# 23 rounded weight slabs written by casting DMAs, and ScalarE's place for what is left, in a hybrid decoder layer

## The chip, the core and the metric

The kernel runs on one core of one Trainium2 chip, as one program without communication. The metric is the device time in microseconds (us); the lower the better. The engines are named as the profile names them: PE is TensorE, DVE is VectorE, ACT is ScalarE, POOL is GpSimd, SP is SyncE.

## What is computed

One decoder layer on 512 tokens of width 1024, all in float32 from outside. The normalised input goes through one wide projection; an HGRN2 recurrence and a sparse attention work on parts of it; their results are lifted, gated, summed and projected out; a squared-ReLU MLP of width 4096 and a last norm follow.

```python
h = rms_norm(x, attn_norm_g[l])
proj = h @ w_in[l]
(hq, hf, hi, hg, cq, ak, av, ik, iw, gate_a, gate_b) = jnp.split(proj, splits, axis=-1)
oa = hgrn2_mixer(hq, hf, hi, lbs[l])
...
cq = rms_norm(cq, q_norm_g[l])
aq = cq @ w_uq[l]
iq = cq @ w_iq[l]
ob = dsa_mixer(aq, iq, iw, ak, av, layer_norm(ik), rel_bias)
mix = jax.nn.sigmoid(gate_a) * (oa @ w_up_hgrn[l]) + jax.nn.sigmoid(gate_b) * (ob @ w_up_attn[l])
x = x + mix @ w_o[l]
```

## The kernel before

**Slabs.** All weights lie in DRAM as one stream of slabs of 128 x 1024 float32 (512 KB). `PLAN` lists the first 55 by kind: hf (slabs 0 to 3), hq (4 to 7), c0 (8 to 11), c1 (12), hi (13 to 16), iq (17), hg (18 to 21), ga (22, 23), uq (24), ga (25 to 30), ua (31 to 34), gb (35 to 42), ub (43 to 46), wo (47 to 54). The MLP's slabs follow in a loop of their own, which the change leaves as it is but for one count of a semaphore.

**Three products per weight.** A matmul in the type float32r sees only a rounded operand. To keep float32's precision each operand is split in a rounded part and a rest, and PE forms hi x hi, hi x lo and lo x hi: 24 matmuls of 512 columns for a slab (of 384 for iq). So each slab n needs, besides the slab itself in `raw`, its rounded form `whi` and the rest `wlo` = raw - whi. There are four buffers of each (`SLOTS`), slab n in number n % 4.

**Who splits.** SP loads `raw` (`load`); for slab n it waits until the split of slab n - 4 is done. ACT copies raw to whi with a cast, in `hi(n)`, once PE is through with slab n - 4 (`used_up`). For most slabs DVE then subtracts (`lo`). For the 23 slabs of `BY_DMA` (18 to 40: hg, ga, uq, ua, and gb 0 to 5) ACT also writes wlo = -whi, in the same `hi(n)`, and POOL issues a DMA that adds raw into wlo (`split_by_dma`). PE waits for that DMA (`split_done`) before its first matmul of the slab.

**Order.** Every engine's program is written out by hand and runs in order; semaphores alone tie the engines together. All walk n over the 55 slabs, and each slab has four parts. In slab n, ACT runs `hi(n + 3)` at part `HI_PART[n]` (0 for n up to 29, 1 from 30), and in each part first empties the banks of that part (`evict`), then does the side work woven into it (`do_side`). POOL begins step n with `split_by_dma(n + 2)` and goes on with its side work of slab n.

```python
HI_PART = [0 if n < n_ua - 1 else 1 for n in range(NPLAN)]
...
for n in range(NPLAN):
    split_by_dma(n - 1 + AHEAD)
    for s in side[n]:
        do_side(s)
```

**Side work that matters here.** In slabs 18 to 21 the indexer: PE writes a bank, ACT turns it to `rel`, DVE adds it into `sc`. In slabs 19 to 23 the recurrence's output: ACT writes `hO` (slabs 20 to 23, one chunk each), and when ACT is through with the slab it squares the chunk (`out_squares`, four squares into `junk`); POOL waits for these squares in its step of that slab to form a reciprocal root (two operations on `small`). Slabs iq and uq fill all four banks of the projections; ACT writes two halves of `iqs` or `aqs` from each bank, DVE the other two, and only then is the bank free for the next slab. In slab 23 ACT starts a DMA of 1 MB (`bt`), ahead of the negation that the change puts there. From slab 30 to 40 attention units are woven in: POOL writes the bias `bm` of a unit, PE forms the unit's logits, DVE adds bm into `tt`, ACT takes the exponential of tt, PE transposes it two units later. bm has two buffers and tt three.

Of the kernel before, what the change touches and what calls it, by code (L numbers as in the profile page):

```python
# [46 lines left out]
SLOTS = 4  # L47
AHEAD = 3


PLAN = ([("hf", j) for j in range(4)] + [("hq", j) for j in range(4)] + [("c0", j) for j in range(4)]
        + [("c1", 0)] + [("hi", j) for j in range(4)] + [("iq", 0)]
        + [("hg", j) for j in range(4)] + [("ga", 0), ("ga", 1), ("uq", 0)] + [("ga", j) for j in range(2, 8)] + [("ua", j) for j in range(4)]
        + [("gb", j) for j in range(8)] + [("ub", j) for j in range(4)] + [("wo", j) for j in range(8)])
NPLAN = len(PLAN)
# [19 lines left out]
def build(nc, x, slabs, vecs, consts, onehot, rel_bias, final_g, out):  # L75
    with ExitStack() as ctx:
# [6 lines left out]
        def sem(name):  # L83
            return ctx.enter_context(nc.semaphore(name))
# [3 lines left out]
        whi = [place(f"whi{s}", 16 + 4 * s, SLAB, F32R) for s in range(SLOTS)]  # L88
# [97 lines left out]
        raw_in = [sem(f"raw_in{s}") for s in range(SLOTS)]  # L186
        br_in = {k: sem(f"br_in{k}") for k in br}
        hi_done, lo_done, lod_done, slab_used = sem("hi_done"), sem("lo_done"), [sem(f"lod_done{q}") for q in range(SLOTS)], sem("slab_used")
        full = [sem(f"full{b}") for b in range(8)]
        free = [sem(f"free{b}") for b in range(8)]  # L190
        const_in, fg_in, y_in, out_done = sem("const_in"), sem("fg_in"), sem("y_in"), sem("out_done")
# [57 lines left out]
        def nextb():  # L249
# [5 lines left out]
        n_hq, n_hi, n_hg, n_ga, n_ua, n_gb, n_ub, n_wo = (  # L255
            AT_SLAB[k, 0] for k in ("hq", "hi", "hg", "ga", "ua", "gb", "ub", "wo"))
# [83 lines left out]

        PARTS = 4
        PART_OF = {"turn": 1, "decay_k": 0, "exp_k": 3, "decay_q": 3, "use_k": 3, "use_q": 2}
        HI_PART = [0 if n < n_ua - 1 else 1 for n in range(NPLAN)]
        LO_PART = [0 if n < n_ua - 1 else 2 for n in range(NPLAN)]
        woven = {}
        for n in range(NPLAN):
# [3 lines left out]
            seen, p, top = 0, 0, 0  # L350
            for s in side[n]:
                if s in BK:
                    p = (2 * seen + 1) * PARTS // (2 * count)
# [25 lines left out]
        BY_DMA = range(n_hg, n_gb + 6)  # L379
        NLO = NPLAN - len(BY_DMA) - 1  # L380

        def split_done(n):

            if n == 1:
                return S["lo1_done"], 1
            if n in BY_DMA:
                return lod_done[n % SLOTS], 16 * len([m for m in BY_DMA if m <= n and m % SLOTS == n % SLOTS])
            return lo_done, n + 1 - sum(m in BY_DMA or m == 1 for m in range(n))

        def used_up(n):  # L390

            if n in by_count:
                return slab_used, by_count[n]
            b, u = c1_bank if tiles[n] == "side" else tiles[n][-1]
            return full[b], u + 1
# [3 lines left out]
        WPB = 4 + len(PRODUCTS)  # L399
# [153 lines left out]
        def _(pool):  # L553
# [29 lines left out]
            for l in range(LEVELS):  # L583
                B, H = 2 << l, 1 << l
                m = mskb[:, 64 * l:64 * l + 64]
# [5 lines left out]
            def do_side(s):  # L591
# [31 lines left out]
                if s[0] == "attn" and s[1] < NU:  # L623
# [13 lines left out]
                    if far:  # L637
# [2 lines left out]
                    pool.tensor_tensor(bm[u % 2][:, far:w], bt3[:, h, WIN - (w - far):WIN], sc_of(i)[:, far:w],  # L640
                                       ALU.add).then_inc(S["bm_done"], 1)

            def split_by_dma(n):

                if n in BY_DMA:
                    s = n % SLOTS
                    pool.wait_ge(S["neg_done"], n - BY_DMA[0] + 1)
                    pool.dma_start(wlo[s][:, :].bitcast(F32), raw[s][:, :], accum_op=ALU.add).then_inc(lod_done[s], 16)

            for n in range(NPLAN):  # L650
                split_by_dma(n - 1 + AHEAD)
                for s in side[n]:
                    do_side(s)
# [21 lines left out]
        def _(act):  # L675
            def hi(n):

                s = n % SLOTS
                act.wait_ge(raw_in[s], 16 * (n // SLOTS + 1))
                if n >= SLOTS:  # L680
                    act.wait_ge(*used_up(n - SLOTS))
                act.copy(whi[s][:, :], raw[s][:, :]).then_inc(hi_done, 1)  # L682
                if n in BY_DMA:
                    act.wait_ge(hi_done, n + 1)
                    act.activation(wlo[s][:, :], whi[s][:, :].bitcast(F32), ACT.Copy, scale=-1.0).then_inc(S["neg_done"], 1)  # L685

            def wait_full(bu):
# [209 lines left out]
            for n in range(NPLAN):  # L897
                for p in range(PARTS):
                    if p == HI_PART[n]:
                        hi(n + AHEAD)  # L900
                    evict(n, p)
                    for s in woven[n][p]:
                        do_side(s)
                for s in side[n]:
                    if s[0] == "out":
                        out_squares(s[1])
# [100 lines left out]
        def _(dve):  # L1007
            def lo(n):

                s = n % SLOTS  # L1010
                dve.wait_ge(hi_done, n + 1)
                dve.tensor_tensor(wlo[s][:, :], raw[s][:, :], whi[s][:, :].bitcast(F32),  # L1012
                                  ALU.subtract).then_inc(lo_done, 1)

# [341 lines left out]
            def lo_op(q, src, it):  # L1356

                s = (NPLAN + q) % SLOTS
                dve.wait_ge(hi_done, it * WPB + (NPLAN + q + 1))
                dve.tensor_tensor(wlo[s][:, :], src[:, :], whi[s][:, :].bitcast(F32), ALU.subtract).then_inc(lo_done, 1)  # L1360

            def lo_in(m, it):
# [565 lines left out]
```

## Time and profile before

| | |
|---|---|
| median of 3 runs | 741.98 us (741.24 to 742.3) |
| the profiled execution, its own time | 742.13 us |
| its span in the profile | 740.4 us |
| PE matmul busy | 720.3 us (97%), 3490 instructions |
| DVE / ACT / POOL busy | 511.4 / 380.3 / 107.5 us |
| granted TensorE clock | 0.998 |
| all 16 DMA engines, bytes | 85.12 MB, 115 GB/s in the mean |

The engines' busy times add up to far more than the span, since they work at once; what counts is which of them the others wait for in a given stretch. The span is 1.7 us shorter than the device time of the same execution. PE's matmuls are pipelined: each is shown as 390 ns long, but one of 512 columns starts every 227 ns, so that 24 take 5.45 us. Starts, not ends, are to be compared.

### The profile page before, as it was taken

Reading aid. Unit: us, or ns where it says so; the run is one execution under the profiler, and the core shown is the slowest. Engines: PE = TensorE matmul, PEld = TensorE weight load, DVE = VectorE, ACT = ScalarE, POOL = GpSimd, SP = SyncE. Lnnn points to the kernel's source line nnn. Section 1 sums busy time; section 2 is a strip of 40 time slices with the busy share of each in tenths; the row PEclk is TensorE's granted clock in tenths of the full one; section 3 lists DMA queues with packets and bytes.
Section 4 is the critical chain, followed back from the end, with each engine's and each line's share of the span. In section 5 each row is a group of like instructions: output and inputs, shape, how many; then the busy total and the mean of one; then the engine's idle time right before and its main releaser. Section 6 shows DMA issues by size and latency. Waiting matters only on the chain.

```text
span 740.4 us, 9813 instructions
## 1 busy us (share of the span) xinstructions
PE 720.3 (97%) x3490; PEld 604.0 (82%) x3490; DVE 511.4 (69%) x791; ACT 380.3 (51%) x595; POOL 107.5 (15%) x145
## 2 busy tenths in 40 slices
PE   5999999999999999999999999999999999999996
PEld 4788878788788888888888888888888888888885
DVE  4676996658798852336635696868768595968964
ACT  6463645877755666443313654545363544545442
POOL 3421241012213356200200100000000000000002
PEclk9999999999999999999999999999999999999999
DMA  8456124524977544112722333241505052332102
GB/s 296 145 100 154 58 91 102 133 74 100 257 184 171 143 114 114 58 58 85 256 86 81 147 114 113 86 142 57 170 11 198 17 156 70 113 114 85 30 1 113
DMA packets 25051, 85.12 MB, mean 115 GB/s; under 512 B 2712, under 2 KB 4920, under 8 KB 25016
## 3 DMA queue, kind: packets, MB, share of 16 engines
q1 hardware_dynamic: 19104, 67.87, 27.1%
q0 software_dynamic: 3312, 12.06, 8.7%
q10 hardware_dynamic: 2600, 4.72, 2.9%
q8 instruction: 22, 0.36, 0.2%
q14 instruction: 13, 0.11, 0.0%
HBM read 68.91 MB, written 3.67 MB: 98 GB/s over the span
## 4 chain that ended last, share of the span: by engine, by line
PE 93%; ACT 4%; DVE 1%; issue 1%; DMA 0%; POOL 0%; POOLq 0%; SPq 0%; ACTq 0%; DVEq 0%
PE bank L1513 19%; PE bank L1514 19%; PE bank L1515 19%; PE bank L1559 8%; PE bank L1563 8%; PE bank L1560 8%; PE bank L1744 2%; PE bank L1521 2%; PE bank L1652 2%; PE bank L1530 1%; PE bank L1726 1%; ACT whi L682 1%; PE bank L1725 1%; ACT wlo L685 1%; ACT iqs L744 0%
## 5 line engine op out<-in xcount | busy, mean ns | idle before, releaser
L1513 PE MATMUL bank<-hTh,whi 128*128 128x512 f32 (+1 forms) x264 | 102.9, 390 | 0.5 <-DVE hTl L1038 0.5
L1515 PE MATMUL bank<-hTh,wlo 128*128 128x512 f32 (+1 forms) x264 | 102.8, 389 | 0.0
L1514 PE MATMUL bank<-hTl,whi 128*128 128x512 f32 (+1 forms) x264 | 102.8, 389 | 0.0
L682 ACT CAST whi<-raw 128x1024 fp32r<-128x1024 f32 x58 | 60.4, 1042 | 41.2 <-PE bank L1515 40.6
L1559 PE MATMUL bank<-hTh,whi 128*128 128x512 f32 x192 | 77.8, 405 | 2.2 <-DVE aqs L1068 1.5
L1515 PE MATMUL bank<-whi,al 128*128 128x512 f32 x196 | 76.3, 389 | 0.0
L1514 PE MATMUL bank<-wlo,ah 128*128 128x512 f32 x196 | 76.3, 389 | 0.0
L1513 PE MATMUL bank<-whi,ah 128*128 128x512 f32 x196 | 76.3, 389 | 0.0
L1563 PE MATMUL bank<-hTl,whi 128*128 128x512 f32 x192 | 75.1, 391 | 0.0
L1560 PE MATMUL bank<-hTh,wlo 128*128 128x512 f32 x192 | 74.9, 390 | 0.0
L1012 DVE TENSOR_TENSOR wlo<-raw,whi 128x1024 fp32r<-128x1024 f32 x34 | 45.3, 1335 | 26.1 <-ACT whi L682 26.1
L927 ACT ACTIVATE rt<-bank 128x512 f32<-128x512 f32 x32 | 19.2, 599 | 85.8 <-PE bank L1515 85.8
L1513 PEld LDWEIGHTS bank<-hTh,whi 128*128 128x128 f32 (+1 forms) x264 | 49.2, 186 | 11.4 <-issue 0.7
L1515 PEld LDWEIGHTS bank<-hTh,wlo 128*128 128x128 f32 (+1 forms) x264 | 49.2, 186 | 10.7
L1514 PEld LDWEIGHTS bank<-hTl,whi 128*128 128x128 f32 (+1 forms) x264 | 49.2, 186 | 10.6
L918 ACT CAST whi<-raw 128x1024 fp32r<-128x1024 f32 x29 | 29.8, 1049 | 50.3 <-PE bank L1515 50.3
L1360 DVE TENSOR_TENSOR wlo<-br,whi 128x1024 fp32r<-128x1024 f32 x32 | 39.1, 1222 | 18.8 <-ACT whi L923 18.6
L665 POOL TENSOR_SCALAR small<-small 128x1 f32<-128x1 f32 x4 | 0.8, 191 | 310.0 <-ACT junk L697 310.0
L1393 DVE TENSOR_TENSOR acc<-bank,acc 128x512 f32<-128x512 f32 x70 | 45.1, 688 | 0.0
L1559 PEld LDWEIGHTS bank<-hTh,whi 128*128 128x128 f32 x192 | 36.2, 189 | 9.7 <-issue 3.4
L1513 PEld LDWEIGHTS bank<-whi,ah 128*128 128x128 f32 x196 | 36.8, 188 | 7.7
L1515 PEld LDWEIGHTS bank<-whi,al 128*128 128x128 f32 x196 | 36.8, 188 | 7.6
(245 smaller groups left out, 1623.6 us busy)
## 6 DMA issues: line engine op xcount, KB each, us to landing
raw<-slabs SPq DMA_DIRECT2D x87, 512.0 KB, 3.4
br<-slabs SPq DMA_DIRECT2D x32, 512.0 KB, 3.4
wlo<-raw POOLq DMA_DIRECT2D x23, 512.0 KB, 4.6
xs<-x SPq DMA_DIRECT2D x4, 512.0 KB, 5.3
y<-x ACTq DMA_DIRECT2D x1, 2048.0 KB, 8.9
bias_rows<-rbias ACTq DMA_DIRECT2D x1, 1536.0 KB
out<-ys SPq DMA_DIRECT2D x3, 512.0 KB, 2.6
bt<-bias_rows ACTq DMA_DIRECT2D x1, 1024.0 KB, 6.0
```

The source lines that it names most:

```text
L682: act.copy(whi[s][:, :], raw[s][:, :]).then_inc(hi_done, 1)
L918: act.copy(whi[s][:, :], raw[s][:, :]).then_inc(hi_done, 1)
L927: act.activation(rt[m % 2][:, :], bank[m][:, :], ACT.Relu).then_inc(free[m], 1)
L1012: dve.tensor_tensor(wlo[s][:, :], raw[s][:, :], whi[s][:, :].bitcast(F32), ALU.subtract).then_inc(lo_done, 1)
L1360: dve.tensor_tensor(wlo[s][:, :], src[:, :], whi[s][:, :].bitcast(F32), ALU.subtract).then_inc(lo_done, 1)
L1393: dve.tensor_tensor(a_, bank[b][:, :], a_, ALU.add).then_inc(free[b], 1)
L1513: pe.matmul(dst, lh, rh, start=start, stop=False)
L1514: pe.matmul(dst, lh, rl, start=False, stop=False)
L1515: return pe.matmul(dst, ll, rh, start=False, stop=stop)
L1559: pe.matmul(dst, wh[:, k, c0:c0 + P], hi_[:, k, t0:T], start=k == 0, stop=False)
L1560: pe.matmul(dst, wl[:, k, c0:c0 + P], hi_[:, k, t0:T], start=False, stop=False)
L1563: ins = pe.matmul(dst, wh[:, k, c0:c0 + P], lo_[:, k, t0:T], start=False, stop=k == kt - 1)
```

## The change

For the 23 slabs of `BY_DMA` ACT no longer casts. POOL issues a DMA that reads the slab a second time from DRAM and writes it to whi, with a cast from float32 to float32r (`round_by_dma`), at the start of its step n for slab n + 3, before `split_by_dma(n + 2)`. It may start once PE is through with slab n - 1. ACT's negation is a step of its own (`neg`), now at the end of the last part of slab n, and waits for the casting DMA (`cast_done`). The accumulating DMA also waits for `raw_in`. `HI_PART` is 3 for iq and uq. The slabs 20 and 27, which it would place there, are among the 23, so that this part of the diff moves nothing by itself: what takes the cast and the negation from ahead of these banks is the new `neg`. The counts of `hi_done` go down by the 23 casts.

```diff
--- before.py
+++ after.py
@@ -186,6 +186,7 @@
         raw_in = [sem(f"raw_in{s}") for s in range(SLOTS)]
         br_in = {k: sem(f"br_in{k}") for k in br}
         hi_done, lo_done, lod_done, slab_used = sem("hi_done"), sem("lo_done"), [sem(f"lod_done{q}") for q in range(SLOTS)], sem("slab_used")
+        cast_done = [sem(f"cast_done{q}") for q in range(SLOTS)]
         full = [sem(f"full{b}") for b in range(8)]
         free = [sem(f"free{b}") for b in range(8)]
         const_in, fg_in, y_in, out_done = sem("const_in"), sem("fg_in"), sem("y_in"), sem("out_done")
@@ -340,7 +341,8 @@
 
         PARTS = 4
         PART_OF = {"turn": 1, "decay_k": 0, "exp_k": 3, "decay_q": 3, "use_k": 3, "use_q": 2}
-        HI_PART = [0 if n < n_ua - 1 else 1 for n in range(NPLAN)]
+        HI_PART = [3 if PLAN[n][0] in ("iq", "uq") else 0 if n < n_ua - 1 else 1 for n in range(NPLAN)]
+        NEG_PART = [3] * NPLAN
         LO_PART = [0 if n < n_ua - 1 else 2 for n in range(NPLAN)]
         woven = {}
         for n in range(NPLAN):
@@ -384,8 +386,15 @@
             if n == 1:
                 return S["lo1_done"], 1
             if n in BY_DMA:
-                return lod_done[n % SLOTS], 16 * len([m for m in BY_DMA if m <= n and m % SLOTS == n % SLOTS])
+                return lod_done[n % SLOTS], of_dma(n)
             return lo_done, n + 1 - sum(m in BY_DMA or m == 1 for m in range(n))
+
+        def of_dma(n):
+            return 16 * len([m for m in BY_DMA if m <= n and m % SLOTS == n % SLOTS])
+
+        def rounded(n):
+
+            return hi_done, n + 1 - sum(m in BY_DMA for m in range(n))
 
         def used_up(n):
 
@@ -640,14 +649,23 @@
                     pool.tensor_tensor(bm[u % 2][:, far:w], bt3[:, h, WIN - (w - far):WIN], sc_of(i)[:, far:w],
                                        ALU.add).then_inc(S["bm_done"], 1)
 
+            def round_by_dma(n):
+
+                if n in BY_DMA:
+                    s = n % SLOTS
+                    pool.wait_ge(*used_up(n - SLOTS))
+                    pool.dma_start(whi[s][:, :], slabs[n]).then_inc(cast_done[s], 16)
+
             def split_by_dma(n):
 
                 if n in BY_DMA:
                     s = n % SLOTS
                     pool.wait_ge(S["neg_done"], n - BY_DMA[0] + 1)
+                    pool.wait_ge(raw_in[s], 16 * (n // SLOTS + 1))
                     pool.dma_start(wlo[s][:, :].bitcast(F32), raw[s][:, :], accum_op=ALU.add).then_inc(lod_done[s], 16)
 
             for n in range(NPLAN):
+                round_by_dma(n + AHEAD)
                 split_by_dma(n - 1 + AHEAD)
                 for s in side[n]:
                     do_side(s)
@@ -675,13 +693,19 @@
         def _(act):
             def hi(n):
 
+                if n in BY_DMA:
+                    return
                 s = n % SLOTS
                 act.wait_ge(raw_in[s], 16 * (n // SLOTS + 1))
                 if n >= SLOTS:
                     act.wait_ge(*used_up(n - SLOTS))
                 act.copy(whi[s][:, :], raw[s][:, :]).then_inc(hi_done, 1)
+
+            def neg(n):
+
+                s = n % SLOTS
                 if n in BY_DMA:
-                    act.wait_ge(hi_done, n + 1)
+                    act.wait_ge(cast_done[s], of_dma(n))
                     act.activation(wlo[s][:, :], whi[s][:, :].bitcast(F32), ACT.Copy, scale=-1.0).then_inc(S["neg_done"], 1)
 
             def wait_full(bu):
@@ -901,6 +925,8 @@
                     evict(n, p)
                     for s in woven[n][p]:
                         do_side(s)
+                    if p == NEG_PART[n]:
+                        neg(n + AHEAD)
                 for s in side[n]:
                     if s[0] == "out":
                         out_squares(s[1])
@@ -1008,7 +1034,7 @@
             def lo(n):
 
                 s = n % SLOTS
-                dve.wait_ge(hi_done, n + 1)
+                dve.wait_ge(*rounded(n))
                 dve.tensor_tensor(wlo[s][:, :], raw[s][:, :], whi[s][:, :].bitcast(F32),
                                   ALU.subtract).then_inc(lo_done, 1)
 
@@ -1356,7 +1382,7 @@
             def lo_op(q, src, it):
 
                 s = (NPLAN + q) % SLOTS
-                dve.wait_ge(hi_done, it * WPB + (NPLAN + q + 1))
+                dve.wait_ge(hi_done, it * WPB + (NPLAN - len(BY_DMA) + q + 1))
                 dve.tensor_tensor(wlo[s][:, :], src[:, :], whi[s][:, :].bitcast(F32), ALU.subtract).then_inc(lo_done, 1)
 
             def lo_in(m, it):
```

**Moved on ACT, slabs 23 to 25.** In these rows `whi_53` to `whi_56` are buffers 0 to 3, `wlo_57` to `wlo_60` likewise, so that slab 25 is whi_54, slab 26 whi_55, slab 27 whi_56. Before:

```order
L847 ACTIVATE hO<-bank 128x512
L853 DMA bt<-bias_rows 128x8x256
L767 ACTIVATE tha<-bank 128x512
L697 ACTIVATE junk,small<-hO 128x128 x4
L682 CAST whi_56<-raw_52 128x1024
L685 ACTIVATE wlo_60<-whi_56 128x1024
L744 ACTIVATE aqs_67<-bank 64x512 x4
L744 ACTIVATE aqs_68<-bank 64x512 x4
```

After the change (lines 709, 721, 768, 791, 871 and 877 are 685, 697, 744, 767, 847 and 853 of before):

```order
L871 ACTIVATE hO<-bank 128x512
L877 DMA bt<-bias_rows 128x8x256
L791 ACTIVATE tha<-bank 128x512
L709 ACTIVATE wlo_59<-whi_55 128x1024
L721 ACTIVATE junk,small<-hO 128x128 x4
L768 ACTIVATE aqs_67<-bank 64x512 x4
L768 ACTIVATE aqs_68<-bank 64x512 x4
L709 ACTIVATE wlo_60<-whi_56 128x1024
```

The cast of slab 26 and 27 is gone. The negation of slab 26 stood ahead of slab 23's work and now stands after it, ahead of the four squares; that of slab 27 went from ahead of the eight writes of aqs to behind them.

**Moved on POOL, steps 23 to 30.** `raw_49` to `raw_52` are the buffers 0 to 3 of raw; the rows on small are the reciprocal roots. Before, from the two rows on small of slab 23 on:

```order
L564 TENSOR_SCALAR small<-small 128x4
L565 TENSOR_TENSOR small<-small 128x4
L648 DMA wlo_59<-raw_51 128x1024
L648 DMA wlo_60<-raw_52 128x1024
L648 DMA wlo_57<-raw_49 128x1024
L648 DMA wlo_58<-raw_50 128x1024
L648 DMA wlo_59<-raw_51 128x1024
L648 DMA wlo_60<-raw_52 128x1024
L648 DMA wlo_57<-raw_49 128x1024
L640 TENSOR_TENSOR bm_104<-bt,sc 128x128
```

After the change, from the same two rows on, as far as slab 29:

```order
L573 TENSOR_SCALAR small<-small 128x4
L574 TENSOR_TENSOR small<-small 128x4
L657 DMA whi_56<-slabs 128x1024
L665 DMA wlo_59<-raw_51 128x1024
L657 DMA whi_53<-slabs 128x1024
L665 DMA wlo_60<-raw_52 128x1024
L657 DMA whi_54<-slabs 128x1024
L665 DMA wlo_57<-raw_49 128x1024
L657 DMA whi_55<-slabs 128x1024
L665 DMA wlo_58<-raw_50 128x1024
```

Ahead of each accumulating DMA there is now a casting one, of the slab after it, on the same queue.

## Rows read from the trace of the kernel before

**Rows 1.** The page's first part: busy us (share) xinstructions of each engine.

```profile
PE 720.3 (97%) x3490; PEld 604.0 (82%) x3490; DVE 511.4 (69%) x791; ACT 380.3 (51%) x595; POOL 107.5 (15%) x145
```

**Rows 2.** Waits of PE: line waited for, us in total, times, longest.

```profile
PE bank L1559 <- DVE aqs L1068: 1.5, 1, 1.5
PE bank L1513 <- DVE iqs L1068: 1.1, 1, 1.1
PE bank L1642 <- ACT hKT L839: 1.1, 1, 1.1
...
PE bank L1642 <- ACT rel L806: 0.5, 1, 0.5
```

**Rows 3.** Timeline of ACT, 112 to 156 us: start, length, line, operation.

```profile
131.25 1.06 ACT L685 ACTIVATE wlo<-whi 128x1024 fp32r<-128x1024 f32 x1
132.21 1.99 ACT L744 ACTIVATE iqs<-bank 64x384 fp32r<-64x384 f32 x4
...
146.23 1.04 ACT L682 CAST whi<-raw 128x1024 fp32r<-128x1024 f32 x1
...
148.26 0.58 ACT L839 ACTIVATE hKT<-bank 128x512 f32<-128x512 f32 x1
```

**Rows 4.** Timeline of ACT, 152 to 214 us, slabs 21 to 26.

```profile
176.28 0.18 ACT L697 ACTIVATION_READ_ACCUMULATOR junk<-hO 128x1 f32 x1
...
181.23 0.60 ACT L847 ACTIVATE hO<-bank 128x512 f32<-128x512 f32 x1 [1.19 <-PE bank L1705]
...
183.38 0.19 ACT L697 ACTIVATION_READ_ACCUMULATOR junk<-hO 128x1 f32 x1
...
192.62 4.89 ACT L744 ACTIVATE aqs<-bank 64x512 fp32r<-64x512 f32 x8
```

**Rows 5.** Timeline of POOL, 170 to 345 us; L648 issues the accumulating DMA.

```profile
176.56 0.65 POOL L564 TENSOR_SCALAR small<-small 128x4 f32<-128x4 f32 x1 [10.04 <-ACT junk L697]
...
178.54 0.91 POOL L648 DMA_DIRECT2D wlo<-raw  x1
...
190.77 0.19 POOL L564 TENSOR_SCALAR small<-small 128x4 f32<-128x4 f32 x1 [4.93 <-ACT junk L697]
...
192.04 1.83 POOL L648 DMA_DIRECT2D wlo<-raw  x2
```

**Rows 6.** DMA issues of the page: count, KB each, median us from issue to landing.

```profile
raw<-slabs SPq DMA_DIRECT2D x87, 512.0 KB, 3.4
wlo<-raw POOLq DMA_DIRECT2D x23, 512.0 KB, 4.6
```

**Rows 7.** DMA queues of the page: packets, MB, share of 16 engines (q1 SP's, q0 POOL's).

```profile
q1 hardware_dynamic: 19104, 67.87, 27.1%
q0 software_dynamic: 3312, 12.06, 8.7%
```

**Rows 8.** All of L648's 23 issues: ns min, median, max.

```profile
L648 POOL DMA_DIRECT2D wlo<-raw x23: 852/874/1108, 115.8 to 287.2; - x23
```

**Rows 9.** Stretches: PE, PEld, DVE, ACT, POOL busy (x), PEclk, DMA share, GB/s.

```profile
186.00:214.00 28.00, 26.51 (x130) 22.06 (x129) 22.46 (x60) 19.30 (x33) 5.52 (x7) 1.00 0.98 243
```

**Rows 10.** Timeline of PE: first matmuls of slabs 25 and 30.

```profile
195.38 0.47 PE L1559 MATMUL bank<-hTh,whi 128*128 128x512 f32 x1 [1.49 <-DVE aqs L1068]
...
224.45 0.39 PE L1559 MATMUL bank<-hTh,whi 128*128 128x512 f32 x1
```

**Rows 11.** Timeline of PE, DVE and POOL in attention, slabs 35 and 36.

```profile
273.28 0.34 PE L1725 MATMUL bank<-kdh,aqs 128*128 128x384 f32 x1
...
280.49 0.49 PE L1521 MATMUL bank<-cst,tt 128*128 128x128 f32 x3
...
273.84 0.56 DVE L1308 CUSTOM_DVE_ANT_0 tt<-bank,bm 128x384 f32<-128x384 f32 x1 [0.77 <-PE bank L1726]
...
268.10 0.88 POOL L648 DMA_DIRECT2D wlo<-raw  x1
...
269.84 0.73 POOL L640 TENSOR_TENSOR bm<-bt,sc 128x256 f32<-128x256 f32 x1
```

## The prediction

> **What bounds the kernel now.** I read the page first: PE is busy 97% of the span [rows 1]. So nothing the change does can pay unless it shortens a wait of PE, and nothing it does costs unless it makes one. The waits of PE come next [rows 2]: besides its start, PE waits for something inside the first 55 slabs in only a few places. Four of them lie where the change works: 1.1 us at the start of slab 18, for banks that iq filled (iqs); 0.5 us and 1.1 us in slabs 19 and 20, for ACT's rel and hKT; 1.5 us at the start of slab 25, for the banks that uq filled (aqs). That is 4.2 us, the most that can be won. The timeline of ACT shows why: a cast and a negation of 1.04 and 1.06 us stand right ahead of iqs at 132.21 and ahead of hKT at 148.26 [rows 3]. In the attention slabs PE has no wait at all, so ACT's freed time is worth nothing there.
>
> The DMA side is the second thing to read. A slab loaded by SP needs 3.4 us from issue to landing, an accumulating DMA 4.6 us [rows 6]. How long they hold the 16 DMA engines comes from the queues [rows 7]: 8.7% of 740.4 us over 23 transfers is 2.8 us each; 27.1% over 67.87 MB is 1.55 us for 0.524 MB, say 1.6. The accumulation reads two operands, and costs nearly twice as much. From 186 to 214 us these engines are already 98% busy [rows 9].
>
> **What the change removes.** 23 casts by 1.04 us leave ACT, 24 us; all but a few lie beside PE's work. In slabs 17 to 20 they don't: ahead of iqs one cast goes and the negation that stays has been moved forward to slab 16's end, so the banks come 1.1 us earlier or more; ahead of the first rel the cast and the negation go together or shrink by half. I take 2.5 us of the 2.7 us of PE's waits there (1.1, 0.5, 1.1), since DVE's own chain of iqs, hK, hQ and sc is next in line. Bounds: 1.1 (DVE takes over at once) and 2.7. From slab 21 on everything is then 2.5 us earlier.
>
> **What it adds: the price of a casting DMA.** No row shows one. It reads DRAM once and writes SBUF once, like SP's load; it is issued by POOL, which takes 0.87 us for it [rows 8]. The lower bound is a load: 3.4 us to landing, 1.6 us of the DMA engines; if conversion has the accumulation's price, 4.6 and 2.8 us. I take 1.6 us of the engines, because the accumulation's doubled time goes with its doubled reads, which a cast doesn't have, and 3.8 us to landing (3.4, and 0.4 more for POOL's slower issue). The Trainium skill, page "DMA: Bandwidth & Descriptors", section "Anatomy of one DMA — SWDGE (gpsimd) path", fits a DMA of GpSimd by 2.0 us and the bytes over 436,000 per us; as an estimate from that page this transfer would take 3.2 us, and the sum would be some 1.2 us lower, at 741.3 us.
>
> **The new ring of waits, slabs 21 to 24.** This is the part that the diff hides. ACT is in order, and its negation, now ahead of the four squares, waits for the casting DMA. POOL is in order too: it issues the next casting DMA only after its reciprocal root, which waits for those squares. So cast, negation, squares, root, next cast form a ring: 3.8 + 1.06 + 1.7 (hO's end at 181.83 to the last square's at 183.57 [rows 4]) + 1.3 (190.77 to 192.04 [rows 5]) = 7.9 us, against 5.45 us of matmuls and 1 to 2 us of side work for a slab on PE. Followed through:
> - The squares of slab 21 ended at 176.46 [rows 4]. 2.5 us earlier, with the negation now ahead of them, 175.0. POOL needed 2.0 us from the start of small at 176.56 to its DMA at 178.54 [rows 5], so slab 25's cast is issued at about 176.9 and lands at 180.7. ACT has written hO by 179.3 and waits 1.4 us. Negation to 181.8, squares to 183.5, slab 26's cast issued at 184.8.
> - It lands at 188.6, and about 1 us later because ACT's 1 MB transfer bt starts at the same time: 189.6. Negation to 190.7, squares to 192.4, and only then aqs, which began at 192.62 [rows 4].
>
> So the banks of uq come free 0.2 to 0.3 us earlier than before, and slab 25 starts at about 195.1 and not at 195.38 [rows 10]: the change clears the cast out of the way of the query banks, and the wait for the DMA takes its place. Of the 2.5 us that PE had gained nearly all is given back here. With the bounds of the DMA's price (3.4 and 4.6 us, twice in the ring) slab 25 starts between 194.3 and 196.7.
>
> **The DMA engines, slabs 25 to 30.** PE takes 29.1 us from slab 25 to slab 30 (195.38 to 224.45 [rows 10]), with no other work but one group of transposes. In the same time POOL's queue must bring, in order, five casts (slabs 27 to 31, each ahead of the accumulation of the slab before) and five accumulations (26 to 30), while SP brings five slabs: 5 x (1.6 + 2.8 + 1.6) = 30.0 us. The first cast is issued at about 193.7 and moves data from some 0.8 us later, at 194.5; the last accumulation has landed at 224.9, where PE stood at its first matmul at 224.45. So PE loses about 0.5 us against before by slab 30. Earlier ones are in balance within a few tenths. From slab 31 a slab lasts over 7 us and the queue catches up. At the other end, with 2.8 us for a cast, the round takes 7.2 us, five take 36, and slab 30 comes at 231 us, 6.5 us late.
>
> **Attention, slabs 30 to 40.** POOL may not start its step before PE has finished the slab before, since the casting DMA waits for its buffer. Before, it issued slab 38's accumulation at 268.10, 5.2 us ahead of the slab's first logits at 273.28, and bm was ready 2.5 us after that issue, at 270.57 [rows 11]. Now the step begins at 271.9 (six matmuls ahead of those logits), cast and negation let the accumulation go between 272.8 and 275, bm is ready at 275.3 to 277.5 and DVE's tt, which ran at 273.84, at 276 to 278. PE wants this unit's transposes at 280.49 [rows 11]; ACT's exponential takes about 1 us. It is hidden, with 1.5 us to spare; if that cover fails, each of 10 slabs costs a few tenths, at most 1 us.
>
> The Trainium skill, page "SBUF — State Buffer", section "Who interferes with whom", says that VectorE in its two-port modes locks GpSimd out while it writes descriptors, which speaks against 23 more of POOL's DMAs. Here 23 issues took 852 to 1108 ns beside a busy DVE [rows 8], so the trace gives the rule at most 0.25 us per issue, and it changes no sum.
>
> **The sum.** Won 2.5 us up to slab 21, given back 2.2 us by slab 25, lost a further 0.8 us by slab 30 (from 0.3 early to 0.5 late), nothing after it: +0.5 us. Against the profiled execution's own 742.13 us (span 740.4 and 1.7 around it) that is 742.6; the median of the runs is 0.15 us lower, so 742.5 us.
>
> **The rivals.**
> - *The DMA engines become the bound.* If a cast costs them as much as an accumulation, slabs 25 to 30 run at 7.2 us each: 6.5 us late, and 7 with slab 31, about 749 us. For it: 98% busy already [rows 9]. Against it: the doubled time of the accumulation has another reason, its second read. It decides from about 1.7 us per cast upward, and costs about 5 us for each us above that.
> - *The gain stays.* If casts land in 3.4 us or less, POOL is never late, and slabs queue up enough ahead, PE keeps 2.5 us and perhaps the 1.5 us at slab 25: 738 to 740 us, say 739. For it: accumulations now land 4 us and more ahead of their use. Against it: the ring has no slack in slabs 22 to 24. (With the Trainium skill's fit for a DMA of GpSimd, named above, this rival and the forecast would be equally likely.)
> - *Late bm.* On top of the forecast, attention's slabs lose 0.2 to 0.4 us each through POOL's late step: 745 us.
> - *The cast rounds nothing.* If the DMA merely copied the bits, whi would hold the whole weight and wlo zero. The time would be that of the lower bound, 741 to 742 us; it lies within my forecast's own range.
>
> **Numbers.** What a measurement here can tell from no change is about 0.2%, 1.5 us. Forecast (741 to 744): 0.37. DMA engines as the bound (744 to 751): 0.33. Gain kept (738 to 740.5): 0.20. Late bm (743 to 746): 0.10. From the forecast's case 0.27 falls within 0.2%, 0.05 on either side; with the others, faster 0.24, same 0.27, slower 0.49. The likeliest single case gives 742.5 us. The range leaves out about one in ten at each end: 739.2 to 750.0 us; the forecast alone would have 740.5 to 744.
>
> **What would show it.** ACT's L709 waits for a DMA in slabs 22 to 24, and aqs starts within 1 us of 192.6. PE's waits for iqs, rel and hKT are gone or halved, that for aqs is there still. The casts' share of q0 gives the price: 17.4% of the span in all would mean 2.8 us each, 13.7% means 1.6. PE waits for the DMA wlo<-raw at slabs 26 to 30, under 1 us in the sum by the forecast, 5 us or more by the first rival. The forecast is wrong if aqs starts before 190.5, if PE waits for DMAs over 2 us, or if PE waits in attention.

## The result and the profile after

The change makes the kernel slower: 754.18 us (median of 4 runs, 753.26 to 755.34) against 741.97 us beside it (741.24 to 742.3). The ratio is 1.0168, with a 95% interval of 1.0151 to 1.0185. The profiled execution took 753.3 us with a span of 751.5, so it lost 11.1 us of span to the one before.

Where it was lost can be read off PE alone. The table gives the start of each slab's first matmul in the timeline of PE, before, and how much later (+) or earlier (-) it comes in the changed kernel and in two runs that are told below.

| slab | before, us | changed | negation late alone | casts 18 to 23 alone |
|---|---|---|---|---|
| 18 (hg) | 134.49 | -1.14 | -0.66 | -1.23 |
| 21 | 161.55 | -3.32 | -0.71 | -3.39 |
| 24 (uq) | 188.28 | -3.35 | -0.71 | -3.31 |
| 25 | 195.38 | -2.16 | -0.70 | -4.96 |
| 26 | 200.90 | -0.37 | -0.66 | -5.04 |
| 32 (ua) | 238.27 | -0.23 | -0.66 | -5.04 |
| 33 | 245.48 | +1.43 | +0.50 | -5.04 |
| 34 | 253.50 | +7.41 | +4.72 | -5.04 |
| 35 (gb) | 261.75 | +7.92 | +5.49 | -5.04 |
| 36 | 271.81 | +10.49 | +10.83 | -5.04 |
| 41 | 321.91 | +10.87 | +11.17 | -5.04 |

The offset of a whole execution is not exact: in the second run, which changes nothing before slab 30, slab 18 comes 0.66 us early all the same. Differences between rows of one column don't have this fault. From slab 18 to 21 PE wins 2.18 us in the changed kernel and 2.16 with casts for 18 to 23, and nothing to speak of with the negation late.

So PE wins 3.35 us up to slab 24, gives 3 back by slab 26, and loses 11 us from slab 32 on, nearly all in 32, 33 and 35. The first two stretches were foreseen in kind; the third was not. The page after, busy times and queues (against [rows 1] and [rows 6, 7]):

```profile
PE 725.9 (97%) x3490; PEld 606.6 (81%) x3490; DVE 512.0 (68%) x791; ACT 355.5 (47%) x572; POOL 120.5 (16%) x168
...
q1 hardware_dynamic: 19104, 67.87, 26.5%
q0 software_dynamic: 6624, 24.12, 13.7%
...
whi<-slabs POOLq DMA_DIRECT2D x23, 512.0 KB, 4.8
wlo<-raw POOLq DMA_DIRECT2D x23, 512.0 KB, 6.0
```

The 23 casting DMAs doubled q0's bytes and took its share from 8.7% to 13.7%: 103.0 us less the 64.4 of the accumulations, over 23, is 1.7 us of the DMA engines each. PE's share is still 97%, which shows how little that number says. PE's waits after, to be held against [rows 2]:

```profile
PE bank L1770 <- ACT ob L907: 3.0, 2, 2.9
PE bank L1585 <- DMA wlo<-raw: 2.7, 1, 2.7
PE bank L1547 <- ACT et L893: 1.9, 5, 0.5
PE bank L1751 <- DVE small L1334: 1.1, 2, 0.7
```

The waits for iqs, hKT, rel and aqs are gone. New are one for an accumulating DMA (slab 25) and three kinds inside attention: for ob, for et and for tt's bank. These three sum to 6.0 us. Held matmul by matmul against before, the steps in which PE waited grew by 7.5 us, since a wait listed as 0.5 us can move the next start by 0.7. A further 3 us are the clock, which shows in the windows (PE, PEld, DVE, ACT, POOL busy, granted clock, DMA share, GB/s):

```profile
246.00:254.00 8.00, 6.36 (x34) 4.99 (x33) 4.39 (x12) 3.07 (x10) 2.89 (x6) 1.00 0.73 188
254.00:262.00 8.00, 6.21 (x21) 5.47 (x22) 6.77 (x18) 2.23 (x7) 1.93 (x3) 0.57 0.61 154
262.00:270.00 8.00, 8.00 (x49) 7.00 (x48) 4.26 (x13) 2.80 (x7) 3.62 (x5) 1.00 0.47 105
```

A mean clock of 0.57 over 8 us means 6.8 us at 1.2 GHz instead of 2.4. PE worked in 6.2 of them, and matmuls of 512 columns started every 0.427 us instead of every 0.227, so that about 3 us were lost. The clock fell during PE's wait of 2.9 us (at 255.19 us; the wait ended at 255.79), and it is in nobody's list of waits: PE counts as busy meanwhile. About 0.7 us of the 11 are spread over many small steps.

The clock fell once before, in slab 25, which is easily overlooked:

```profile
193.00:200.00 7.00, 6.78 (x23) 5.48 (x24) 6.71 (x14) 3.13 (x5) 1.70 (x3) 0.76 1.03 273
```

It stood at 1.2 GHz from 193.75 to 197.16 us, just after the wait of 2.7 us for slab 25's accumulation, and slab 25 took 7.31 us instead of 5.52. That is where the last 1.8 us of the 3 given back show. The clock is not their only cause, though: slab 26's accumulation landed at 200.49 us and PE began the slab at 200.53, so a faster slab 25 would have ended in a wait.

What keeps PE waiting in attention is seen on the other engines, whose waits from 230 us on are these after:

```profile
ACT tt L899 <- DVE small L1334: 43.7, 23, 4.2
POOL wlo L665 <- ACT wlo L709: 33.0, 8, 5.4
DVE tt L1334 <- issue: 31.9, 9, 4.8
...
DVE tt L1334 <- PE bank L1752: 9.9, 6, 2.5
```

Before, the same view read:

```profile
DVE tt L1308 <- PE bank L1726: 32.2, 18, 3.6
...
POOL wlo L648 <- ACT wlo L685: 13.1, 7, 2.6
...
ACT tt L875 <- DVE small L1308: 6.6, 8, 2.0
```

DVE used to wait for PE, as it should in a kernel bound by PE. Now it waits mostly for something that the profile calls "issue", with nobody named; the timeline shows what. Slabs 32 and 33, POOL first, then ACT and DVE:

```profile
238.06 0.59 POOL L657 DMA_DIRECT2D whi<-slabs  x1 [1.08 <-PE bank L1589]
244.00 0.88 POOL L665 DMA_DIRECT2D wlo<-raw  x1 [5.35 <-ACT wlo L709]
244.58 2.15 POOL L649 TENSOR_TENSOR bm<-bt,sc 128x128 f32<-128x128 f32 x3
...
252.35 0.87 POOL L665 DMA_DIRECT2D wlo<-raw  x1 [5.11 <-ACT wlo L709]
252.93 2.40 POOL L649 TENSOR_TENSOR bm<-bt,sc 128x256 f32<-128x256 f32 x3
```

```profile
242.25 0.40 ACT L899 ACTIVATE tt<-tt,small 128x128 f32<-128x128 f32 x1 [1.54 <-DVE small L1334]
242.56 0.18 ACT L899 ACTIVATION_READ_ACCUMULATOR tt<-tt,small 128x1 f32 x1
242.65 1.04 ACT L709 ACTIVATE wlo<-whi 128x1024 fp32r<-128x1024 f32 x1
```

```profile
245.49 0.29 DVE L1334 CUSTOM_DVE_ANT_0 tt<-bank,bm 128x128 f32<-128x128 f32 x1 [3.01 <-issue]
```

The casting DMA goes out at 238.06. POOL then stands 5.35 us for the negation of slab 34, which ACT does at 242.65, since it is last in its slab and comes behind the exponential at 242.25. Only at 244.58 does POOL write the bm of slab 32's units, three in a row; DVE, idle for 3 us, gets its bm at 245.49. bm has two buffers, so POOL can never be more than a unit or two ahead; a late bm makes tt late, tt the exponential, the exponential the negation, and the negation the next slab's bm. It is a ring of waits through three engines, and PE drops into it.

### The profile page after: what moved, and what is told of

Its sections match the earlier page's. It is cut to its first block, busy times and chain, and to the rows that moved or that the text cites. A ratio compares the mean times of both kernels' runs of the same rounds, so it can differ in the third digit from the quotient of the medians.

```text
span 751.5 us, 9813 instructions
## 1 busy us (share of the span) xinstructions
PE 725.9 (97%) x3490; PEld 606.6 (81%) x3490; DVE 512.0 (68%) x791; ACT 355.5 (47%) x572; POOL 120.5 (16%) x168
## 3 DMA queue, kind: packets, MB, share of 16 engines
q0 software_dynamic: 6624, 24.12, 13.7%
q10 hardware_dynamic: 2600, 4.72, 2.9%
## 4 chain that ended last, share of the span: by engine, by line
PE 61%; issue 2%; DVE 1%; POOL 1%; ACT 1%; POOLq 0%; ACTq 0%
PE bank L1539 17%; PE bank L1540 17%; PE bank L1541 17%; PE bank L1585 3%; PE bank L1589 3%; PE bank L1586 3%; PE bank L1770 2%; PE bank L1547 1%; PE bank L1752 0%; PE bank L1751 0%; POOL bm L649 0%; DVE tt L1334 0%; PE bank L1793 0%; DVE hTl L1064 0%; ACT wlo L709 0%
## 5 line engine op out<-in xcount | busy, mean ns | idle before, releaser
L702 ACT CAST whi<-raw 128x1024 fp32r<-128x1024 f32 x35 | 36.4, 1043 | 37.0 <-PE bank L1541 36.4
L944 ACT CAST whi<-raw 128x1024 fp32r<-128x1024 f32 x29 | 29.8, 1052 | 50.3 <-PE bank L1541 50.3
L1334 DVE CUSTOM_DVE_ANT_0 tt<-bank,bm 128x128 f32<-128x128 f32 (+3 forms) x32 | 15.5, 487 | 45.4 <-issue 31.9
```

## The experiments

Each ran beside the kernel before on the same chip. The ratio is that of the run to the kernel before.

**Casts for slabs 18 to 30 only.** From slab 31 ACT casts and negates at its old place.

```diff
+        CASTS = range(n_hg, n_ua)
...
-                if n in BY_DMA:
+                if n in CASTS:
...
+                if n in BY_DMA:
+                    act.wait_ge(*rounded(n))
+                    act.activation(wlo[s][:, :], whi[s][:, :].bitcast(F32), ACT.Copy, scale=-1.0).then_inc(S["neg_done"], 1)
```

> The change for slabs 18 to 30 only; slabs 31 to 40 get ACT's cast and negation at part 1 as before. Theory A (all of the 12 us is lost in the attention slabs, through POOL's order, and nothing up to slab 31, where PE stood 0.3 us earlier than before): 741 to 742.5 us, PE never waits from slab 31 on. Rival B (the DMA engines, full from 186 to 240 us, are the cause and the attention slabs only show it late): 744 us or more, with waits of PE left near slab 32 or 33.

Measured: 741.77 us, ratio 1.0003 (0.9994 to 1.0012), and PE has no wait from slab 31 on. The whole loss lies in the attention slabs. Up to slab 31 the casts win and lose as in the change: PE stands 4.46 us early at slab 24 and 0.57 at slab 26, with the clock at 1.2 GHz for 3.4 us in slab 25 here too. Its waits there:

```profile
PE bank L1592 <- DVE aqs L1101: 2.7, 1, 2.7
...
PE bank L1592 <- DMA wlo<-raw: 0.9, 1, 0.9
```

**The negation late, and nothing else.** The kernel before, without a casting DMA; for slabs 33 to 40 the negation stands at the last part, where the change has it.

```diff
                 act.copy(whi[s][:, :], raw[s][:, :]).then_inc(hi_done, 1)
+                if n in BY_DMA and n < n_ua + 2:
+                    neg(n)
+
+            def neg(n):
...
+                    if p == PARTS - 1 and n + AHEAD >= n_ua + 2:
+                        neg(n + AHEAD)
```

> The kernel before, without any casting DMA, but with the negations of slabs 33 to 40 at the last part of the slab, behind the exponentials, where the change has them. Theory A (the late negation in front of POOL's bm is the cause by itself): slower, 747 to 754 us, with PE waiting in slabs 32 to 36. Rival B (the cause is the DMA traffic or the wait for the buffer): 741.5 to 743.5 us.

Measured: 753.54 us, ratio 1.0153 (1.0137 to 1.0168), with the losses in the same slabs (table above). This is the strongest run of the study: one moved instruction per slab, no DMA added, and the whole slowdown is there. The waits of all its engines, over the whole run, show the same three members (before, the first was 60.8 us and the second 8.3):

```profile
POOL wlo L648 <- ACT wlo L691: 96.0, 16, 9.5
...
ACT tt L881 <- DVE small L1316: 35.8, 20, 3.3
DVE tt L1316 <- issue: 31.3, 8, 4.8
```

PE's listed waits in attention are 6.8 us, and the clock fell twice, for 3.4 us each time:

```profile
250.00:260.00 10.00, 7.57 (x36) 6.36 (x35) 6.64 (x17) 3.60 (x10) 3.00 (x4) 0.83 0.43 106
...
270.00:280.00 10.00, 7.25 (x35) 5.50 (x35) 3.98 (x14) 5.96 (x14) 6.08 (x9) 0.91 0.42 105
```

**bm ahead of the accumulating DMA.** The change, all 23 casts and the late negation included; only POOL's order is another.

```diff
                 round_by_dma(n + AHEAD)
-                split_by_dma(n - 1 + AHEAD)
+                if n < n_ua - 1:
+                    split_by_dma(n - 1 + AHEAD)
                 for s in side[n]:
                     do_side(s)
+                if n >= n_ua - 1:
+                    split_by_dma(n - 1 + AHEAD)
```

> The change, but from step 30 on POOL does its side work (bm) between the casting DMA and the accumulating one, so that bm no longer stands behind the wait for ACT's negation. Theory A (POOL stands 5 us per slab waiting for a negation that is now at the end of the slab, bm is late, and DVE, ACT and PE follow): 741.5 to 744 us, the waits of PE for et, ob and tt gone. Rival B (the wait of the casting DMA for PE's release of the buffer is what holds POOL): little change, 751 to 755 us. Rival C (DMA engines): little change too.

Measured: 742.3 us, ratio 1.0013 (1.0001 to 1.0025). PE waits for nothing in attention; of its new waits only that of slab 25 is left:

```profile
PE bank L1588 <- DMA wlo<-raw: 2.8, 1, 2.8
```

The clock falls in slab 25 as in the change (193.56 us, for 3.4 us). So the late negation does no harm on ACT; it does it through what stands behind it on POOL.

**The wait for the buffer alone.** The kernel before, with POOL waiting for PE's release of the slab before in steps 30 to 37, as a casting DMA makes it.

```diff
             for n in range(NPLAN):
+                if n >= n_ua - 1 and n + AHEAD in BY_DMA:
+                    pool.wait_ge(*used_up(n - 1))
                 split_by_dma(n - 1 + AHEAD)
```

> The kernel before, with one wait added: in steps 30 to 37 POOL waits, before the accumulating DMA, for PE's release of the slab before, as the casting DMA makes it. No casting DMA, negations where they were. Rival B alone: if that wait costs, 744 us or more. Theory A: the negation is long done, POOL loses at most 1 to 2 us per slab and PE does not notice, 741.5 to 742.5 us.

Measured: 741.96 us, ratio 0.9997 (0.9988 to 1.0006). No slab moves by more than 0.1 us against its neighbours. This wait, on which my step on attention rested, costs nothing.

**The negation at part 1 in attention.**

```diff
-        NEG_PART = [3] * NPLAN
+        NEG_PART = [3 if n < n_ua - 1 else 1 for n in range(NPLAN)]
```

> The change with the negation in the attention slabs (steps from 30) at part 1, where cast and negation stood before, instead of at the last part. Theory A (late negation): POOL's wait goes, 741.5 to 744 us; but the casting DMA is issued only when the step begins and lands 4 to 6 us later, after part 1, so ACT itself may wait 1 to 3 us a slab for it, ahead of its exponentials: then 744 to 750 us. Rival (buffer release holds POOL): 751 us or more.

Measured: 744.29 us, ratio 1.0038 (1.0025 to 1.005). Ten of the twelve us come back, two fewer than with bm first. ACT now waits 13.6 us for the casts (6.7 us in the changed kernel):

```profile
ACT wlo L709 <- DMA whi<-slabs: 13.6, 9, 3.0
```

In attention that costs PE a single wait, of 0.7 us at the end of slab 30. The waits for two accumulations are those of slabs 25 and 26, ahead of what this run changes:

```profile
PE bank L1585 <- DMA wlo<-raw: 4.5, 2, 2.4
...
PE bank L1547 <- ACT et L893: 0.7, 1, 0.7
```

The profiled execution, of 743.04 us, is the fastest of the five, so it does not show all of what the median lost. It is worth a look at slab 26 all the same. Here the clock did not fall in slab 25, and PE waited 2.1 us for slab 26's accumulation, until 200.35 us, where the changed kernel came at 200.53 on the slow clock and without a wait. In slab 25 the slow clock only filled a wait that was coming.

**The query banks first, alone.** The kernel before, with the changed line for `HI_PART` and nothing else. In the change itself this line does nothing.

```diff
-        HI_PART = [0 if n < n_ua - 1 else 1 for n in range(NPLAN)]
+        HI_PART = [3 if PLAN[n][0] in ("iq", "uq") else 0 if n < n_ua - 1 else 1 for n in range(NPLAN)]
```

> The kernel before with one line of the change alone: the cast and negation of slabs 20 and 27 go to the last part of iq and uq, behind the banks that ACT empties; no casting DMA. Theory A (the waits of PE for iqs and aqs were ACT's cast and negation standing ahead of them): these two waits, 1.1 and 1.5 us, go or nearly so, rel and hKT stay, 739.5 to 741 us. Rival B (the cast of the next slabs only falls on other waits, since ACT has the same work): 741.5 to 742.5 us.

Measured: 740.51 us, ratio 0.9976 (0.9967 to 0.9985): faster, by 1.8 us by the ratio and 1.4 by the medians. The waits for iqs and aqs are both gone, but a part falls on rel, since ACT has the same work as before ahead of the first of them; it does slab 20's cast and negation later, at 133.26 us, between two of the iqs banks:

```profile
PE bank L1642 <- ACT rel L806: 1.7, 1, 1.7
```

**Casts for slabs 18 to 23 only.** As the first run, with `CASTS = range(n_hg, n_uq)`. ACT casts and negates slab 27, and here the changed `HI_PART` does put that behind the uq banks.

> Casting DMAs for slabs 18 to 23 only (hg and the first two ga); from slab 24 ACT casts and negates as before, with slab 27's behind the uq banks. Up to slab 24 the change won 3.4 us, and by slab 26 it had given 3 us back. Theory D (it is given back because casts, accumulations, loads and bt together overfill the DMA engines from 183 to 205 us): without the casts of slabs 24 to 27 the 3.4 us stay and the wait for aqs shrinks as in the run with the query banks first, 736.5 to 739 us, faster than both kernels. Rival (ring: it is given back because ACT's negation, ahead of the squares, waits for the cast in slabs 22 and 23, a wait which here is still there for no slab past 20): the same time would come out, so this run prices the loss and does not name it. If the gain does not stay, 740 to 742 us, something else takes it, such as ACT or DVE themselves.

Measured: 737.36 us, ratio 0.9935 (0.9923 to 0.9948): faster than both kernels. All 3.3 us stay, aqs starts at 187.3 us, and PE has no wait from slab 18 to the end of attention. The 1.65 us that come at slab 25 are not the work of the casting DMAs: the run before, with the line for `HI_PART` alone, won 1.65 us at the same place.

**Why the gain goes in slabs 24 and 25.** Two candidates: the ring of cast, negation, squares, root and next cast; and DMA engines that are full. Two runs on top of bm first. One moves the 1 MB transfer bt out of the way:

```diff
-        file(max(n_hg + 3, n_ch + NT), ("bt", ))
+        file(n_ua - 3, ("bt", ))
```

> The change with bm first (742.3 us), and with the 1 MB transfer bt issued in slab 28 instead of slab 23. It tells theory D (DMA engines overfull: bt took 10.4 us from issue to landing in the changed kernel, in the midst of the accumulations of slabs 25 and 26, which landed 0.04 us before PE started) from the ring (negation ahead of the squares, POOL's root, next cast). Theory D: slab 25's accumulation lands 2 to 3 us earlier and PE keeps 1.5 to 3 us, 739.5 to 741 us, unless bt then delays slabs 29 to 31. Ring: no change at slab 25 and 26, 742 to 743 us.

Measured: 749.48 us (742.59 to 752.42), ratio 1.0091 (1.0057 to 1.0124). A miss, and a poor design: bt took 19.5 us to land among the casts of slabs 31 to 33, and PE lost 6.7 us at slab 30. Its accumulation took 10.8 us to land, the clock fell, and POOL's bm waited for bt:

```profile
232.53 1.43 POOL L649 TENSOR_TENSOR bm<-bt,sc 128x128 f32<-128x128 f32 x3 [8.67 <-DMA bt<-bias_rows]
```

What it still tells is slabs 24 and 25: PE gave back 2.8 us between slab 24 and slab 26 there, against 3.1 with bt in its old place. The DMA share from 183 to 205 us fell from 1.01 to 0.86, and slab 25's accumulation landed at 189.32 us instead of 193.05. Yet PE was held at slab 25 just as long, now by aqs, which the ring makes late:

```profile
PE bank L1588 <- DVE aqs L1097: 2.7, 1, 2.7
```

So in the change two things end within 0.4 us of each other at slab 25, the ring's aqs and the accumulation, and taking away one of them shows little.

The other takes the cast out of the way of the squares:

```diff
-                    if p == NEG_PART[n]:
+                    if p == NEG_PART[n] and not any(s[0] == "out" for s in side[n]):
                         neg(n + AHEAD)
                 for s in side[n]:
                     if s[0] == "out":
                         out_squares(s[1])
+                        neg(n + AHEAD)
```

> The change with bm first (742.3 us), and in slabs 20 to 23 ACT squares hO before it waits for the cast and negates, so that POOL's root and next casting DMA no longer wait for the cast before. All 23 casts stay, bt stays in slab 23. Ring (what PE gives back in slabs 24 and 25, 3.1 us, is lost to cast, negation, squares, root, next cast in a circle): aqs begins 1 us or more earlier, slab 25's accumulation lands earlier, PE keeps 1.5 to 3 us, 739.5 to 741 us. DMA engines (over 98% busy there whatever the order): PE still stands at slab 26 where it did, 742 to 743 us.

Measured: 740.61 us, ratio 0.9983 (0.9974 to 0.9992). PE gave back 0.9 us between slabs 24 and 26 instead of 3.1, and the clock did not fall there; so the ring is about two thirds of it. Two waits are left, at slab 25 for aqs and at slab 26 for an accumulation that took 9.1 us to land:

```profile
PE bank L1589 <- DMA wlo<-raw: 1.6, 1, 1.6
...
PE bank L1589 <- DVE aqs L1098: 0.6, 1, 0.6
```

I put this rest down to full DMA engines, but no run shows that by itself: casts for 18 to 23 alone take away the DMAs and the ring together. For 183 to 205 and 205 to 240 us the view by stretches reads, with the squares first:

```profile
183.00:205.00 22.00, 19.82 (x91) 15.94 (x91) 17.61 (x48) 11.50 (x23) 6.24 (x10) 1.00 1.05 292
205.00:240.00 35.00, 35.00 (x181) 29.61 (x180) 30.24 (x82) 15.96 (x37) 13.42 (x22) 1.00 1.00 263
```

and with casts for 18 to 23 alone:

```profile
183.00:205.00 22.00, 22.00 (x102) 18.32 (x102) 18.70 (x51) 16.74 (x28) 5.24 (x7) 1.00 0.96 232
205.00:240.00 35.00, 35.00 (x183) 29.69 (x182) 30.78 (x83) 20.80 (x43) 10.54 (x17) 1.00 0.76 189
```

The DMA share falls from 1.05 to 0.96 in the first stretch and from 1.00 to 0.76 in the second, and PE's 22 us of the first are all busy. (A share over 1 means that the transfers counted to a stretch by their start last beyond its end.)

**The best of both.** Casts for 18 to 23 and 31 to 40, with bm first.

> Casting DMAs for slabs 18 to 23 and again for 31 to 40, with bm first in the attention slabs; ACT casts slabs 24 to 30. If the casts of the attention slabs cost only through POOL's order, which is mended here, the time is that of the casts for 18 to 23 alone, 737 to 738 us, and PE has no wait past slab 25. If they have a price of their own (DMA engines, ACT's wait for the cast), 739 us or more.

Measured: 736.64 us, ratio 0.9924 (0.9911 to 0.9938). It is the fastest median of the study; with 737.36 for the casts of 18 to 23 alone, and overlapping intervals, the two can't be told apart. Casts in attention cost nothing with POOL's order mended, and win nothing.

**The squares first, with casts for 18 to 23.** POOL's order is that of bm first here too.

> Casting DMAs for slabs 18 to 23 only, with the squares of slab 20 ahead of the negation of slab 23 (the only one with both). Nothing waits for these squares that late, so 737 to 738 us, as without; faster than that would mean that ACT's order in slab 20 still costs.

Measured: 737.39 us, ratio 0.9938 (0.9925 to 0.9952): no difference, as expected.

## Why the prediction was wrong

The measured 754.18 us lies above the range (739.2 to 750.0); the forecast was no change, 742.5 us. The step that failed is the one on attention, which was put at nothing. All three signs that the prediction had named against itself came: aqs started before 190.5 (190.25), PE waited over 2 us for a DMA (2.7), and PE waited in attention. Step by step:

- **The gain up to slab 21: right, undersized.** 2.5 us were taken of 2.7; it was 3.3 (3.32 at slab 21), above my upper bound. The bound was the sum of PE's listed waits. Part of a wait hides in a matmul's own duration: from slab 18 to 21 these waits sum to 1.6 us, and PE won 2.18. The start of an execution also varies, by 0.2 and 0.7 us in the two runs that change nothing before slab 30. So such a sum is not a strict bound.
- **The price of a casting DMA: right for the engines, low for the landing.** 1.6 us of the DMA engines were taken, 1.7 measured; q0's share was named as 13.7% and is 13.7%. 3.8 us to landing were taken. In the least crowded cases it landed in 3.6; the median, among other transfers, was 4.8, and the two of the ring, for slabs 25 and 26, took 4.1 and 4.6. The Trainium skill's fit from the page "DMA: Bandwidth & Descriptors", section "Anatomy of one DMA — SWDGE (gpsimd) path", gave 3.2 us as an estimate, which no casting DMA here reached.
- **The ring at slabs 21 to 24: right in kind, and shown by the squares run; its times were about 2 us too late.** ACT waited 0.5 us for slab 25's cast (1.4 expected) and 2.0 us for slab 26's. The squares of slab 21 ended at 173.26 us, not at 175.0, and the later steps kept that lead: aqs began at 190.3 and not at 192.4. Slab 25 came at 193.22 and not at 195.1. DVE had freed its bank at 192.87, and its accumulation, which the step had not followed, landed at 193.18, 9.5 us after its issue. So 1.2 us were given back by slab 25, where 2.2 were forecast.
- **The DMA engines, slabs 25 to 30: right in the sum, wrong in the place.** I had the slabs in balance within a few tenths and 0.8 us lost in all. 1.8 us went at once, in slab 25, with the slow clock and with slab 26's accumulation just in time, and 0.1 after it. The working took 0.8 us from issue to the first data, which stands in no row; in the traces a cast or an accumulation on an empty queue moves its first packet 1.3 to 1.5 us after issue. Slab 30 came 0.26 us early (0.5 late expected). That this is so close is partly luck: a larger gain, less given back by slab 25 and more lost after it nearly cancel. Full engines did not become the bound; the rival that built on them would have shown it here and is refuted, though slower came out.
- **Attention: wrong.** This is the step that failed: "It is hidden, with 1.5 us to spare; if that cover fails, each of 10 slabs costs a few tenths". Three things were wrong in it. I worked it out for slab 36 alone, where the units lie 2.7 us and more apart and where PE indeed never waits; the loss is in slabs 32, 33 and 35, where most units come 2.0 to 2.5 us after the one before and DVE has its maxima besides, in 32 and 33 the gated products too. That the closer spacing is what decides is argued, not tested. I timed the negation by the old trace, within 3 us of the step's start, while the new order puts it behind exponentials that hang on the very bm that waits for it: in slab 32 it began 4.6 us after the slab did. And I left the clock out: about 3 of the 11 us are PE at 1.2 GHz. The late negation alone makes the kernel 11.7 us slower (753.54 beside 741.87), and with bm ahead of the wait for it 742.3 us are measured.
- **The rival "late bm" was this mechanism,** with a chance of 0.10 and a price of 2 to 4 us instead of 11. Its priced cause, POOL's wait for the buffer, costs nothing; the cause is the negation that moved from part 1 to part 3. The diff shows that move in one line, and I followed it through slabs 21 to 24 but not past slab 30.

## What to carry to other kernels

When an instruction moves later on one engine, look at every place where another in-order engine waits for it, and at what is queued behind that wait: here slab 34's product landed at 248.52 us and was first needed at 260.91, with 12 us to spare, but it stood in front of work that was needed at once. Work such a ring through for the slab with the least slack, not for one that is easy to read, and put the wait behind the urgent work. An offload to DMA engines should be made where something waits for the engine that it relieves: six casts of 23 carried the whole 3.3 us that casting DMAs won, and a moved cast and negation of one more slab won the other 1.7.

## What the runs showed of the hardware

- A DMA of 512 KB that reads DRAM and writes SBUF with a cast from float32 to float32r held the 16 DMA engines 1.7 us, like a plain load (1.6) and unlike an accumulation (2.8). POOL took 0.59 us (median) to issue it, against 0.88 for the accumulation.
- With the DMA engines' share at 1.0, the time from issue to landing rose from 3.6 to 9.5 us for a cast and from 4.5 to 9.5 for an accumulation; bt's went from 6.0 to 10.4, and to 19.5 when moved.
- A wait of PE of 2.9 us came with a fall of the granted clock to 0.5 for 6.8 us. The Trainium skill, page "TensorE: Matmul & The Clock Gate", section "HAM oscillation — how this bites in real kernels", says that the clock falls to 1.2 GHz while PE waits for data and that the cost is half of the time spent there. The trace agrees: matmuls of 512 columns started every 0.427 us there and every 0.227 us at 2.4 GHz.
- Waits of 2.7 us (changed kernel) and 2.4 us (negation late) were each followed by 3.4 us at 1.2 GHz, and one of 1.4 us, the last of five within 11 us, too (negation late, 277.62 us). Waits of 1.5 us (before) and of 2.4 and 2.1 us (negation at part 1, slabs 25 and 26) were not. So the length of the last wait alone does not decide it in these runs.
